# A decoder layer whose residual, norm and router step is split into two halves of the row, with the last rows turned back on TensorE

## The reference, cut to what matters

```python
mix = jnp.concatenate([attn, pooled], axis=-1) @ w_out[l]
h = layer_norm(DEEPNORM_ALPHA * h + mix, ln1_g[l], ln1_b[l])
# hier_moe(h):
pg = softmax(t @ w_r1 + b_r1)                 # 4 groups, the best one is taken
lf = (t @ w_r2 + b_r2).reshape(-1, 4, 8)      # 8 experts in that group, the best two are taken
for e in range(N_EXPERTS):                    # 32 experts, 1024 -> 2*256 -> 1024
    a = jax.nn.silu(t @ w_gate[e]) * (t @ w_up[e])
    y = y + combine[:, e:e + 1] * (a @ w_down[e])
h = layer_norm(DEEPNORM_ALPHA * h + ffn, ln2_g[l], ln2_b[l])
```

## Time and profile before

| | us |
|---|---|
| three runs | 545.08, 546.55, 544.93 |
| median | 545.08 |
| the profiled execution's own time | 548.01 |
| span of its trace | 546.3 |

### The profile page before, as it was taken

How to read it: one execution, slowest core, us unless ns; L and a number is a source line. 1 busy time by engine, 2 the same in 40 slices (tenths; PEclk the granted TensorE clock), 3 DMA queues, 4 the chain that set the end, 5 groups by cost and what they waited for, 6 DMA issues and landing times.

```text
span 546.3 us, 6192 instructions
## 1 busy us (share of the span) xinstructions
PE 473.6 (87%) x2210; PEld 274.2 (50%) x2210; DVE 227.7 (42%) x561; ACT 148.7 (27%) x313; POOL 170.3 (31%) x159
## 2 busy tenths in 40 slices
PE   4999999999988998996659999999877789757992
PEld 3587867687744566885624333343333333322341
DVE  2101899999856653538811112121101110101297
ACT  3323433361484673213401111021011110011032
POOL 3153599883354860333420111111111110100000
PEclk9999999999996999998559999899888998979898
DMA  9944469004088004984977999999999999999813
GB/s 313 356 61 51 51 91 390 20 1 154 1 281 297 0 1 125 427 334 175 363 260 304 398 421 421 418 420 421 419 418 422 420 421 418 422 420 386 328 54 154
DMA packets 42440, 148.04 MB, mean 271 GB/s; under 512 B 11284, under 2 KB 15892, under 8 KB 30120
## 3 DMA queue, kind: packets, MB, share of 16 engines
q1 hardware_dynamic: 37992, 139.71, 67.9%
q0 software_dynamic: 4320, 7.82, 3.9%
q10 hardware_dynamic: 96, 0.08, 0.0%
HBM read 137.16 MB, written 18.35 MB: 285 GB/s over the span
## 4 chain that ended last, share of the span: by engine, by line
PE 31%; DVE 25%; DMA 20%; SPq 15%; issue 4%; ACT 3%; POOL 2%; DVEq 0%; ACTq 0%; POOLq 0%
DMA wgu<-in_w_up_dram 10%; PE bank L1499 10%; SPq L497 10%; PE bank L1305 7%; DVE score L946 6%; DVE m L945 5%; DMA xe<-h_rows,row_from 5%; SPq L500 5%; DMA x_again<-in_x_dram 4%; DVE score L963 4%; PE bank L1523 3%; PE bank L1485 2%; PE bank L1348 2%; PE bank L1379 1%; PE bank L1587 1%
## 5 line engine op out<-in xcount | busy, mean ns | idle before, releaser
L1499 PE MATMUL bank<-wgu,xeT 128*64 128x512 f32 x512 | 128.8, 661 | 28.0 <-DMA wgu<-in_w_up_dram 27.1
L1499 PEld LDWEIGHTS bank<-wgu,xeT 128*64 128x64 f32 x512 | 42.9, 151 | 103.5 <-issue 102.4
L1128 DVE TENSOR_TENSOR act_row<-bank,sil 128x256 f32<-128x256 f32 x16 | 6.8, 424 | 152.9 <-ACT sil L857 152.9
L713 POOL DMA_INDIRECT y_rows<-ye,row_to x14 | 14.1, 1008 | 177.9 <-PE bank L1485 117.5
L1523 PE MATMUL bank<-wd,actT 128*64 128x512 f32 x256 | 57.9, 593 | 0.7 <-ACT actT L864 0.7
L620 POOL TENSOR_TENSOR ring_low<-ring,wt_high 128x1024 fp32r<-128x1024 f32 x16 | 38.7, 2416 | 42.9 <-ACT wt_high L740 42.2
L857 ACT ACTIVATE sil<-bank 128x256 f32<-128x256 f32 x16 | 6.1, 383 | 153.7 <-PE bank L1499 153.7
L1523 PEld LDWEIGHTS bank<-wd,actT 128*64 128x64 f32 x256 | 19.7, 137 | 35.6 <-issue 35.6
L1305 PE MATMUL bank<-xT_high,wt_high 128*128 128x512 f32 (+1 forms) x136 | 35.6, 406 | 0.0
L1305 PE MATMUL bank<-xT_low,wt_high 128*128 128x512 f32 (+1 forms) x136 | 35.2, 402 | 0.0
L678 POOL TENSOR_SCALAR lg<-lg,rinv 128x128 f32<-128x128 f32 (+3 forms) x32 | 22.2, 693 | 38.5 <-DVE rinv L1024 38.4
(11 more groups left out here) (199 smaller groups left out, 700.7 us busy)
## 6 DMA issues: line engine op xcount, KB each, us to landing
wgu<-in_w_gate_dram SPq DMA_DIRECT2D x32, 1024.0 KB, 21.7
wgu<-in_w_up_dram SPq DMA_DIRECT2D x32, 1024.0 KB, 26.6
wd<-in_w_down_dram SPq DMA_DIRECT2D x32, 1024.0 KB, 28.7
ring<-in_w_in_dram SPq DMA_DIRECT2D x5, 2048.0 KB, 17.2
wo<-in_w_out_dram SPq DMA_DIRECT2D x2, 2048.0 KB, 7.9
y_rows<-zero SPq DMA_DIRECT2D x1, 4096.0 KB, 21.4
yg<-y_rows SPq DMA_DIRECT2D x8, 512.0 KB, 8.7
bias_rows<-brow SPq DMA_DIRECT2D x1, 2560.0 KB
```

What stands on the lines that cost most here:

```text
L1499: ins = pe.matmul(bank[2 + i][half_rows(n), :], xeT[i][:, k, half_rows(n)], wgu[slots[n]][:, :, k, :], start=k == 0, stop=k == KD - 1)
```

## The change

The residual, the statistics and the norm are done for each half of 512 columns. The output product goes through half 0 and then half 1 in plain order of k, and signals a new semaphore `out_lo_ps` when block k = 3 of half 1 is done. VectorE's loop over t first waits for x, then adds and takes statistics of half 0, then evicts the transposed rows of t-1, then does half 1. ScalarE normalises half 0, VectorE half 1. Transposes, evictions and router matmuls wait for one another by half or by block. For the last tile GpSimd does no gain and offset: TensorE transposes hT back, ScalarE copies the result to h. TensorE multiplies identities into unused PSUM columns at four places (`busy`). The arguments of the exponentials (`gate_biases`) are computed later. SyncE stores tile 3 before it loads expert 4's gate and up, and expert 4's down is loaded after the first gather has landed.

```diff
             def store_h(t):
-                sp.wait_ge(h_ready, t + 1)
+                if t < NT - 1:
+                    sp.wait_ge(h_ready, t + 1)
+                else:
+                    sp.wait_ge(last_h_ready, 2)
                 sp.dma_start(h_dram[P * t:P * t + P, :], h[:, t, :]).then_inc(h_stored, 16)
...
             store_h(2)
+            store_h(3)
             load_gate_up(4, PAIR_SLOTS[2][0], gu_in_slot[PAIR_SLOTS[2][0]])
-            store_h(3)
+            sp.wait_ge(gathered[0], 16)
             load_down(4, PAIR_SLOTS[2][0], down_in_slot[PAIR_SLOTS[2][0]])
-            sp.wait_ge(gathered[0], 16)
             load_expert(5)
...
-            for t in range(NT):
+            for t in range(NT - 1):
                 pool.wait_ge(norm_ready, t + 1)
-                pool.wait_ge(hT_ps, t + 1)
+                pool.wait_ge(norm_hi_ready, t + 1)
+                pool.wait_ge(hT_ps, 2 * t + 2)
...
-                act.activation(rows, rows, ACT.Identity, bias=nmr[:, 0:1], scale=rstd[:, 0:1]).then_inc(norm_ready, 1)
+                act.activation(rows[:, 0:512], rows[:, 0:512], ACT.Identity, bias=nmr[:, 0:1], scale=rstd[:, 0:1]).then_inc(norm_ready, 1)
...
+                if t == NT - 1:
+                    for i in range(2):
+                        act.wait_ge(last_h_ps, i + 1)
+                        act.activation(h[:, t, 512 * i:512 * i + 512], bank[i][:, :], ACT.Copy).then_inc(last_h_ready, 1)
...
+            def residual(t, i):
+
+                hv = h[:, t, 512 * i:512 * i + 512]
+                link(dve.scalar_tensor_tensor(out=hv, in0=x_again[t % 2][i][:, :], scalar=ALPHA, in1=bank[(2 if t % 2 == 0 else 0) + i][:, :],
+                                              op0=ALU.mult, op1=ALU.add))
+                link(dve.bn_stats(stats[:, i, :], hv))
...
                 dve.tensor_scalar(nmr[:, :], mv[:, 0:1], rstd[:, 0:1], -1.0, ALU.mult, ALU.mult).then_inc(scale_ready, 1)
+                dve.wait_ge(scale_ready, k + 1)
+                dve.tensor_scalar(h[:, k, 512:], h[:, k, 512:], rstd[:, 0:1], nmr[:, 0:1], ALU.mult, ALU.add).then_inc(norm_hi_ready, 1)
...
             for t in range(NT):
+                dve.wait_ge(x_again_in[t % 2], 32 * (t // 2 + 1))
+                if t == 0:
+                    dve.wait_ge(out_ps, 1)
+                else:
+                    dve.wait_ge(out_lo_ps, t)
+                residual(t, 0)
                 if t >= 1:
                     transposed_h(t - 1)
                 dve.wait_ge(out_ps, t + 1)
-                dve.wait_ge(x_again_in[t % 2], 32 * (t // 2 + 1))
...
+                residual(t, 1)
                 dve.sem_inc(res_ready, 1)
-                statistics(t, h[:, t, :])
+                statistics()
                 factors(t)
                 if t >= 1:
                     route(t - 1)
+                    gate_biases(t - 1)
...
             def router(t):
-                pe.wait_ge(hT_ready, t + 1)
-                pe.wait_ge(hT_ready_dve, t + 1)
                 if t >= 2:
                     pe.wait_ge(router_sb, t - 1)
-                for k in range(KD):
+                for k in (0, 4, 1, 5, 2, 6, 3, 7):
+                    pe.wait_ge((hT_ready, hT_ready_dve)[k // 4], 4 * t + k % 4 + 1)
...
                 for i in range(2):
-                    for k in (4, 5, 6, 7, 0, 1, 2, 3):
-                        if (i, k) == (1, 7):
+                    for k in range(KD):
+                        if (i, k) == (1, 3):
                             transpose_h(t - 1)
-                        ins = out_product(t, i, k)
+                        ins = out_product(t, i, k, 0, KD - 1)
+                        if (i, k) == (1, 3):
+                            ins.then_inc(out_lo_ps, 1)
...
+            def busy(times, bk=2):
+
+                for i in range(times):
+                    pe.matmul(bank[bk][:, 2 * P:4 * P].rearrange("p (c t) -> p c t", c=2), ident[:, :],
+                              ident[:, :].unsqueeze(1).to_broadcast([P, 2, P]), start=True, stop=True)
+
+            def last_h():
+
+                for k in range(KD):
+                    ins = pe.transpose(bank[k // 4][:, P * (k % 4):P * (k % 4) + P], hT[(NT - 1) % 2][:, k, :], ident[:, :])
+                    if k % 4 == 3:
+                        ins.then_inc(last_h_ps, 1)
+
+            pe.wait_ge(res_ready, NT - 1)
+            busy(4)
             transpose_h(NT - 1)
             pe.wait_ge(res_ready, NT)
             pe.wait_ge(earlier_ready, NT - 1)
             ranks(0, NT - 1, bank[3][:, 0:NE * (NT - 1)]).then_inc(rank_ps, 1)
             router(NT - 1)
+            last_h()
             pe.wait_ge(hot_tok_ready, NT - 1)
             pe.wait_ge(at_rank_ready, 1)
             lists(0, NT - 1)
-            ranks(NT - 1, NT, bank[0][:, 0:NE]).then_inc(rank_ps, 1)
-
+            busy(2, 3)
+            ranks(NT - 1, NT, bank[4][:, 0:NE]).then_inc(rank_ps, 1)
+
+            busy(2, 3)
             pe.wait_ge(earlier_ready, NT)
             pe.matmul(bank[3][:, 0:NE], ones[:, :], earlier[:, NT, :], start=True, stop=True).then_inc(count_ps, 1)
             pe.wait_ge(hot_tok_ready, NT)
             pe.wait_ge(at_rank_ready, 2)
             lists(NT - 1, NT).then_inc(list_ps, 1)
+            pe.wait_ge(last_h_ready, 2)
+            busy(11, 1)
```

More of the change, by code:

```diff
@@ L334, in layer_kernel @@
         h_ready = sem("h_ready")
+        last_h_ps = sem("last_h_ps")
+        last_h_ready = sem("last_h_ready")
         out_ready = sem("out_ready")
@@ L1024, in _, with statistics @@
                     dve.reciprocal(rinv[:, (u - 1) % 8:(u - 1) % 8 + 1], rsum[:, (u - 1) % 8:(u - 1) % 8 + 1]).then_inc(rinv_ready, 1)
-            def statistics(k, rows):
-                for i in range(2):
-                    link(dve.bn_stats(stats[:, i, :], rows[:, 512 * i:512 * i + 512]))
+            def residual(t, i):
[3 more added lines that the diff above has]
+                link(dve.bn_stats(stats[:, i, :], hv))
+            def statistics():
                 link(dve.bn_aggr(mv[:, :], stats[:, :, :]))
@@ L1046, in transposed_h, with gate_biases @@
                 for k in range(KD // 2, KD):
-                    ins = dve.tensor_scalar(hT[t % 2][:, k, :], bank[5][:, P * (k - KD // 2):P * (k - KD // 2) + P],
-                                            gT[:, k:k + 1], bT[:, k:k + 1], ALU.mult, ALU.add)
-                ins.then_inc(hT_ready_dve, 1)
+                    dve.tensor_scalar(hT[t % 2][:, k, :], bank[5][:, P * (k - KD // 2):P * (k - KD // 2) + P],
+                                      gT[:, k:k + 1], bT[:, k:k + 1], ALU.mult, ALU.add).then_inc(hT_ready_dve, 1)
+            def gate_biases(t):
+                link(dve.tensor_scalar(neg[:, t, 0:1], gm8[:, 0:1], -1.0, None, ALU.mult))
+                link(dve.tensor_scalar(neg[:, t, 1:2], em8[:, t, 0:1], -1.0, None, ALU.mult))
+                dve.sem_inc(top_ready, 1)
             def route(t):
@@ L1085, in _ @@
                 dve.wait_ge(out_ps, t + 1)
-                dve.wait_ge(x_again_in[t % 2], 32 * (t // 2 + 1))
-                for i in range(2):
-                    hv = h[:, t, 512 * i:512 * i + 512]
-                    link(dve.scalar_tensor_tensor(out=hv, in0=x_again[t % 2][i][:, :], scalar=ALPHA, in1=bank[(2 if t % 2 == 0 else 0) + i][:, :],
-                                                  op0=ALU.mult, op1=ALU.add))
+                residual(t, 1)
                 dve.sem_inc(res_ready, 1)
-                statistics(t, h[:, t, :])
+                statistics()
                 factors(t)
@@ L1122, in _ @@
             dve.tensor_copy(row_to[:, :], lstf[:, :]).then_inc(row_to_ready, 1)
+            gate_biases(NT - 1)
             def gated(p):
@@ L1371, in weigh_values, with out_product @@
                             ins.then_inc(pv_ps, 1)
-            def out_product(t, i, k):
+            def out_product(t, i, k, first=KD // 2, last=KD // 2 - 1):
                 cols, cols_out = slice(P * t, P * t + P), slice(512 * i, 512 * i + 512)
@@ L1378, in out_product @@
                 for s, (lhsT, rhs) in enumerate(parts):
-                    ins = pe.matmul(bank[(2 if t % 2 == 0 else 0) + i][:, :], lhsT, rhs, start=(k, s) == (KD // 2, 0), stop=(k, s) == (KD // 2 - 1, 2))
+                    ins = pe.matmul(bank[(2 if t % 2 == 0 else 0) + i][:, :], lhsT, rhs, start=(k, s) == (first, 0), stop=(k, s) == (last, 2))
                 return ins
```

32 lines of the change are left out of this document (15 added, 17 removed).

## The result

The changed kernel takes 554.05 us (553.05 to 558.29), the kernel before 545.82 us in the same comparison: ratio 1.0166, interval [1.0124, 1.0207]. It is 8.2 us slower. The prediction said 548.6 us in a range of 543.5 to 551.0: the side is right, the size is not, and the time lies outside the range.

What follows compares the result with a forecast made beforehand. The end was taken to follow the moment the experts' weight stream runs without a gap, set by the chain from tile 2's x to gate_up(0). +7.8 - 2.65 - 0.7 - 0.95 = +3.5 us on 545.08 gave 548.6 us, range 543.5 to 551.0.

Steps and rivals of the forecast that it cites:

- Part 1: VectorE's new order up to the end of tile 3's product: eviction queued behind x, TensorE idle, cold clock; +7.8 us.
- the last router block: Term before tile 3's product: only one router block left after VectorE's eviction of tile 1, 0.45 us at the low clock.
- Part 2: From tile 3's product to its norm: half 0's residual, statistics and most of the eviction run beside the last blocks; -2.65 us.
- Part 3: From tile 3's norm to the first gather: shorter at_rank against added TensorE work; -0.7 us, between -2.1 warm and +0.6 cold.
- cold bound: From tile 3's norm to the first gather with the clock low, TensorE's added work gets in the way: +0.6 us.
- Part 4: From the first gather to the full weight stream: warm transposes and gate_up(0), but expert 4's down queued there; -0.95 us.
- cold to the gather: Rival: clock falls soon after tile 3's norm and only the eleven products raise it; 549.9 to 551 us, chance 0.23.
- The other rivals: Clock holds everywhere (0.12), x lands earlier (0.10), and the new order costs 1 to 2 us more, 550 us (0.08).
- the clock did not hold: Refers to the rival that the clock holds everywhere: -0.1 us, 545.0 us, no change; chance 0.12.
- x did not land earlier on its own: Refers to the rival that tile 2's x lands by 237: -2.4 us, 542.7 us, faster; chance 0.10.

Runs made afterwards that it cites:

- Plain router: Changed kernel with the router's eight blocks in order 0 to 7 instead of 0, 4, 1, 5, ...: 552.04 us, ratio 1.0123.
- No pairs: Changed kernel without the two pairs of identity products around the last ranks; the four and the eleven products stay: 550.68 us, ratio 1.0091.
- Down early: Changed kernel with expert 4's down loaded ahead of the first gather again, right behind its gate and up: 553.21 us, ratio 1.0130.
- x early: Tile 2's x ordered behind expert 0's load instead of expert 2's: in the changed kernel 543.16 us (0.9956), in the kernel before 543.14 us (0.9933).
- evict first: Changed kernel, but VectorE evicts tile 1 before it waits for tile 2's x: 545.68 us, ratio 0.9988.

## Why the prediction was too low, step by step

**Part 1, the mechanism: right.** Eviction behind x, TensorE's gap, the low clock and its length: tile 3's product took 14.2 us (forecast 14.3), and the clock rose 4.6 us after dense work had begun at 244.4 (4.4). The loss goes when one eviction is moved back (0.9988), and most of it comes with the order alone (1.0115, 6.1 of 7.8 us from L to the end).

**Part 1, the router's price: mis-sized.** The step that failed is the term "the last router block (an eighth of 3.6 at the low clock, 0.45)". I read in the diff that router blocks wait one by one, and priced only the last behind the last eviction. But the order 0, 4, 1, 5, ... puts VectorE's first block second, so that 14 of 16 instructions stand behind VectorE's first evicted block and run at the low level: 3.20 us, of which 2.1 reach beyond the eviction (242.31 to 244.41). The product starts at L + 4.9, not L + 3.3. "Plain router" bears this out: with the blocks in plain order it starts at L + 3.65. The product before ended at 251.98 (251.59 and 0.39 us in the earlier trace rows), where I had about 251.8. From there part 1 is +9.1 instead of +7.8.

**Part 2, halves: right.** From the product's end (258.65) to N (261.49) are 2.84 us, forecast 2.85; before they were 5.36, not 5.5. That is -2.5 where I had -2.65.

**Part 3, N to the gather: wrong in sign.** Forecast -0.7; measured +1.5 in the first profile and +3.3 in the second, beyond my cold bound of +0.6. The three `at_rank` fell as forecast, from 2.86 to 0.69 us. But `router(3)` was put at N + 6.2, which fits the same price of one last block, and it ended at N + 8.2 (266.50, 3.21 us at the low clock, again 14 instructions behind VectorE's first block). "Plain router" takes 1.0 of these 2.0 us back; for the rest, `router(3)` stands in TensorE's stream behind the `ranks` of the first three tiles, which waited for VectorE until N + 3.9, and then ran cold. So `route(3)` waited 0.49 us and started 0.8 earlier than before, not 1.4. Then TensorE was late:

```profile
269.51 1.95 PE L1493 MATMUL bank<-ident,hT 128*128 128x128 f32 x8
272.79 2.08 PE L1487 MATMUL bank<-ident 128*128 128x256 f32 x4
274.66 0.47 PE L1472 MATMUL bank<-hsum,tri 128*128 128x32 f32 x2
277.38 5.02 PE L1487 MATMUL bank<-ident 128*128 128x256 f32 x22
```

The choice of tile 3 (`hsum`) was ready at 272.5, 0.8 us sooner after N than before. The last `ranks`, behind transposes, lists and two products, started at 274.66, 2.1 us after it; before they started 0.1 us after it. The gather took 4.41 us against 4.21. That is the +1.5: -0.8, +2.0 and +0.2. The single operations were priced well (transposes 1.97, measured 1.95), the two products less so (1.7, measured 2.08). What made TensorE late is `router(3)`'s 2 us ahead of them: it was free at N + 13.2, not N + 11.4. The second pair of products and the count, priced at +1.1, added nothing in the first profile (from the last `ranks` to the list 3.42 us against 3.41 before) and 0.8 us in the second, where the clock was still low. There the eleven products added another 1.0; the prediction had named this overrun and left it out of the sum. "No pairs" takes 1.2 to 3.0 us of this back. VectorE's half of the norm took 0.55 us in tiles 0 to 2 and 0.80 in tile 3, where it began during GpSimd's memset; the price from the earlier trace rows was 0.44.

**Part 4: small, as forecast, but smaller.** From G for 13.63 us the queue moved 368 GB/s against 267 before, 1.37 MB more, of which 1.05 MB is expert 4's down: 0.32 MB or 0.8 us net, near the -0.95. The end came 0.3 us sooner after G. The difference lies inside what G to the end varies between runs (267.3 to 269.3), so this term can be neither confirmed nor refused. "Down early" fits its two sides: with the down load ahead of the gather as before, G to the end is 3.1 us shorter than in the kernel before, and the moved load takes 2.6 to 2.8 of that back, by single profiles. The gap ahead of the fourth pair's weights, from 287.9 to 291.4 before, is gone as forecast: from 286 to 292 the DMA share is 0.98 or more in every 2 us.

**Sum.** 9.1 - 2.5 + 1.5 - 0.3 = +7.8 us against +3.5. Of the 4.3 missing, 1.3 is part 1, nearly all of it the router's price, 0.1 part 2, 2.2 part 3 and 0.6 part 4. The rival that came nearest is "cold to the gather"; its 549.9 to 551 lacked the same two router terms. In the first profile the clock was back before the eleven products began, in the second only while they ran, as this rival has it. The other rivals fell: the clock did not hold, and x did not land earlier on its own. Made to, with x early, the new order wins 1.4 us from S to N, not the 2.65 of part 2: in the kernel before with x early only 4.2 us lie between the end of the product and N, not 5.5.

The fall of the clock behind N came at 266.1, as `router(3)` was starting and ahead of the eight transposes back; these ran at 0.50. The Trainium skill (TensorE: Matmul & The Clock Gate, Part 4) has it that transposes don't count as activity for the clock as other matmuls do. No run here tests this: in "evict first" the transposes back ran at 1.00 (1.07 us), between other matmuls. Which instructions between N and N + 5 let the clock fall is not settled: four products more ahead of `router(3)` delayed it by 4 us, no run tried the other kinds.

`at_rank` took 2.86 us beside GpSimd's addition and 0.69 without it, and the cast of 128x2 values 1.98 us beside GpSimd's product. The Trainium skill (SBUF — State Buffer, "Who interferes with whom") has it that a VectorE instruction with two SBUF inputs contends with a GpSimd instruction that reads SBUF, and that a cast can run in a two-port mode, in which one of the two engines is blocked for the other's whole instruction. The runs agree; that the cast was in this mode is not shown.

## What to carry to other kernels

When a wait for a late transfer is moved up in an engine's stream, list every later instruction of that stream that another engine needs: here one eviction behind a load cost 6.7 us up to N, and ordering the load behind one expert instead of three was worth 3.6 us in the kernel before and 9 to 11 in the changed one (against its two medians). When several engines produce the blocks of a reduction, price not the last block but all that stand behind the slower producer's first one, at the clock that the gap leaves. Filling products are only worth their place where they stand in idle time; in front of the instruction that ends a chain they are a cost at the low clock (1 to 3 us here, by the profiles).

## What was not expected of the hardware

- From 266.56 to 277 TensorE was busy 10.44 of 10.44 us, with router, transposes, lists and a few identity products, and its granted clock was 0.53 on the mean. From 241.3 on it was back at full after 7.7 us, the last 4.6 of them the dense product of tile 3. In "evict first" the low stretch lasted 6.8 us (253.3 to 260.1), with `router(2)`, the four products and the transposes of tile 3 in it.
- 15 identity products of 256 columns held the clock at 1.00 through a wait of 6 us.
- A cast of 128x2 values took 1.98 us on VectorE beside a GpSimd product, against 0.17 undisturbed (247.53 in the changed kernel): it ended at 247.44, with GpSimd's (247.42).
- An execution's time up to tile 0's residual varied from 207.5 to 211.3 us, between two profiles of the same changed kernel by 1.1; only anchors inside the trace made two profiles comparable.
